# Context rows loaded later, spare matmuls before the head, transposes of a unit one gate tile sooner, gate rows inside the rope part

## The reference

```python
sh, sc, gt = jnp.split(cond @ w_mod[i] + b_mod[i], 3, axis=-1)           # modulation, latent; same for context
h_lat = x * (1.0 + sc[:, None]) + sh[:, None]
h_ctx = ctx * (1.0 + sc_c) + sh_c
q_dn, kv_dn, k_rope, gate = jnp.split(h @ w_in, MLA_SPLITS, axis=-1)     # the "head" (448 columns) and the gate (2048)
q = (_rmsnorm(q_dn, q_norm) @ w_uq).reshape(b, n, MLA_HEADS, MLA_NOPE + MLA_ROPE)
q_pos = jnp.concatenate([qa, _apply_rope(qr, cs[:, None], sn[:, None])], axis=-1)
# 16 heads: scores against 256 latent and 256 context keys, softmax, values, w_uv, times silu(gate), w_out
x = _layernorm(DEEPNORM_ALPHA * x + gt[:, None] * y_lat, ln_g[i], ln_b[i])
```

## Time and profile before

| | |
|---|---|
| median of three runs | 1565.81 us (1564.36 to 1566.65) |
| the profiled execution | 1564.42 us |
| its span, first to last instruction | 1562.5 us |
| mean granted TensorE clock | 0.996 |
| VectorE, ScalarE, GpSimd busy | 56%, 26%, 36% |
| bytes moved by DMA | 272.99 MB, mean 175 GB/s |

### The profile page before, as it was taken

One profiled execution on the slowest core, in us unless ns is written; L12 is line 12 of the kernel. 1 busy time (PEld: TensorE's weight loads), 2 busy tenths in 40 slices (PEclk: granted clock), 3 DMA queues, 4 the chain that ended last, 5 costly groups with the idle time before them and its releaser, 6 DMA issues.

```text
span 1562.5 us, 25477 instructions
## 1 busy us (share of the span) xinstructions
PE 1499.3 (96%) x10192; PEld 1127.4 (72%) x10192; DVE 872.9 (56%) x1745; ACT 402.4 (26%) x956; POOL 565.9 (36%) x412
## 2 busy tenths in 40 slices
PE   4999999999999999999998999999999999999998
PEld 3455556666655568898877888886788874688887
DVE  5879955454578978378576222253533332265642
ACT  1222243333312122332233011000223550232210
POOL 5013340000003303101103977783486201477774
PEclk9999999999999999999999999999999999999999
DMA  9856780130486636838585555554544123455441
GB/s 332 217 182 194 244 269 16 46 116 14 158 259 204 224 136 181 309 136 323 211 304 210 185 175 175 170 183 160 198 162 161 56 108 108 141 178 163 165 148 68
DMA packets 172605, 272.99 MB, mean 175 GB/s; under 512 B 51405, under 2 KB 85304, under 8 KB 171208
## 3 DMA queue, kind: packets, MB, share of 16 engines
q1 hardware_dynamic: 146096, 201.08, 38.1%
q0 software_dynamic: 16512, 42.49, 8.5%
q10 hardware_dynamic: 9880, 27.78, 4.9%
HBM read 228.26 MB, written 42.99 MB: 174 GB/s over the span
## 4 chain that ended last, share of the span: by engine, by line
PE 90%; DMA 4%; DVE 3%; ACT 1%; issue 1%; POOL 0%; SPq 0%; DVEq 0%; ACTq 0%; POOLq 0%
PE bank L499 84%; PE bank L502 6%; DMA memory<-in_w_mod 1%; DMA memory<-mc_scratch 1%; DMA memory<-in_mla_w_in 1%; DMA memory<-in_mla_w_uv 1%; DVE memory L2418 0%; DVE memory L2425 0%; DVE memory L2422 0%; DVE memory L2419 0%; DVE memory L2575 0%; ACT memory L1515 0%; ACT memory L1739 0%; DVE memory L2570 0%; ACT memory L1591 0%
## 5 line engine op out<-in xcount | busy, mean ns | idle before, releaser
L499 PE MATMUL bank<-memory 128*128 128x256 f32 (+8 forms) x9244 | 1402.3, 354 | 38.3 <-DMA memory<-in_w_mod 8.2
L499 PEld LDWEIGHTS bank<-memory 128*128 128x128 f32 (+4 forms) x9244 | 1021.8, 165 | 373.9 <-issue 246.1
L2784 POOL DMA_DIRECT2D mc_scratch<-memory x32 | 28.0, 876 | 498.9 <-DVE memory L2139 441.1
L502 PEld LDWEIGHTS bank<-memory 128*128 128x128 f32 (+1 forms) x948 | 107.9, 141 | 56.9 <-issue 33.6
L502 PE MATMUL bank<-memory 128*128 128x128 f32 (+1 forms) x948 | 124.3, 275 | 21.0 <-ACT memory L1359 9.0
L2823 POOL TENSOR_TENSOR memory<-memory 128x1024 f32<-128x1024 f32 (+1 forms) x34 | 80.9, 2380 | 143.0 <-PE bank L499 95.8
L2809 POOL DMA_DIRECT2D memory<-mc_scratch x32 | 17.3, 543 | 189.3 <-PE bank L499 189.3
L2825 POOL TENSOR_TENSOR memory<-memory 128x1024 f32<-128x1024 f32 (+1 forms) x34 | 81.0, 2382 | 2.7
L2790 POOL DMA_DIRECT2D k_scratch<-memory x128 | 76.5, 630 | 12.7 <-ACT memory L1432 12.3
L2828 POOL TENSOR_TENSOR memory<-memory 128x1024 f32<-128x1024 f32 (+1 forms) x34 | 80.0, 2353 | 2.7
L2826 POOL TENSOR_TENSOR memory<-memory 128x1024 f32<-128x1024 f32 (+1 forms) x34 | 80.5, 2368 | 0.0
(11 more groups left out here) (305 smaller groups left out, 1286.2 us busy)
## 6 DMA issues: line engine op xcount, KB each, us to landing
memory<-in_s_w_glu SPq DMA_DIRECT2D x32, 1024.0 KB, 7.6
memory<-in_w_mod SPq DMA_DIRECT2D x12, 2048.0 KB, 14.1
memory<-in_w_ffn_up SPq DMA_DIRECT2D x22, 1024.0 KB, 7.0
memory<-in_w_in SPq DMA_DIRECT2D x10, 2048.0 KB, 8.0
mc_scratch<-memory POOLq DMA_DIRECT2D x32, 512.0 KB, 4.5
mb_scratch<-memory ACTq DMA_DIRECT2D x32, 512.0 KB, 3.8
memory<-mb_scratch SPq DMA_DIRECT2D x32, 512.0 KB, 6.9
memory<-mc_scratch POOLq DMA_DIRECT2D x32, 512.0 KB, 6.3
```

The costliest lines, as they stand in the source:

```text
L499: return nc.tensor.matmul(o, l, r, start=start, stop=stop, skip_group_check=free)
L502: return nc.tensor.transpose(o, i, ident[0:n, 0:n])
L2784: pool.dma_start(mc_dram[u], over(mc[:, u % 3, GS:GS + 1], (144, 8), (1, P))).then_inc(*S.up("mc_out%d" % (u % 3), u, by=16))
```

## The change

- The two loads of ctx go from ACT's queue to SP's, behind `head_in`. The context's transposes, copies and modulation move behind head tile 0 on TensorE and ScalarE, and behind part of the tables on VectorE. They use banks 0, 1, 6 and 7 in place of the next in turn, which also shifts the banks of what follows; the second transposition of C, into bank 3, now follows the transposed D row there. The transposes of C come after head tile 1 in place of 2.
- `kept_busy(3)` and `kept_busy(5)`: spare products of the identity with 256 columns of x into bank 7, which nothing reads, behind the poles and behind mod column 3.
- Unit u is turned and stored behind gate tile u + 1 in place of u + 2; unit 14 thus comes before mod column 5's transpose.
- The four gate rows of the first layer go from in front of unit 15 into the first rope part. The waits for `ckvT` and `krT` go behind it.
- In the second rope part value product 5 and the latent values of head 6 stand between its steps, in place of behind it.

The core of the diff; ScalarE's program follows TensorE's order in the same way:

```diff
             mod_product(0, 0)
             x_transposes(0, 0)
             mod_product(0, 1)
             mod_turned(0, 0)
-            x_transposes(0, 1)
             mod_product(0, 2)
             mod_turned(0, 1)
             poles_turned()
+            kept_busy(3)
             mod_product(0, 3)
             mod_turned(0, 2)
             mod_turned(0, 3)
+            kept_busy(5)
...
-                if t == 2:
+                if t == 0:
+                    x_transposes(0, 1)
+                if t == 1:
                     for ql in range(2):
                         c_turned(0, ql, 2 + ql)
...
+            def kept_busy(n):
+
+                b = bank(pe, ("busy", n), [], 7)
+                for _ in range(n):
+                    mm(b[:, 0:T], ident, x[:, 0, 0:T], True, True, True)
...
-                    b = bank(pe, ("xT", l, c, k2), [freed], 4 + k2 if l else None)
+                    b = bank(pe, ("xT", l, c, k2), [freed], 4 + k2 if l else ((0, 1, 6, 7)[k2] if c else None))
...
-                if n >= 2:
-                    unit_turned(n - 2)
+                if n >= 1:
+                    unit_turned(n - 1)
...
-            unit_turned(14)
...
-            gate_rows(0)
             unit_turned(15)
             for i in range(2):
                 pe.wait_ge(*S.at("qnT", i))
-            pe.wait_ge(*S.at("ckvT"))
-            pe.wait_ge(*S.at("krT"))
...
                 projected(0)
                 projected(1)
+                if hf == 0:
+                    gate_row(0, 0, 0)
                 plain(0)
                 projected(2)
                 plain(1)
+                if hf == 0:
+                    gate_row(0, 0, 1)
                 rotated(0)
                 projected(3)
+                if hf == 0:
+                    gate_row(0, 1, 0)
+                else:
+                    value_up(H // 2 - 3)
                 plain(2)
+                if hf == 0:
+                    gate_row(0, 1, 1)
                 rotated(1)
+                if hf:
+                    latent_values(H // 2 - 2)
                 plain(3)
...
-                if h >= 2:
+                if h >= 2 and h + 1 != H // 2:
                     value_up(h - 2)
-                if 1 <= h <= H:
+                if 1 <= h <= H and h + 1 != H // 2:
                     latent_values(h - 1)
...
# VectorE
-            for c in range(2):
-                modulated(0, c)
+            modulated(0, 0)
             powers(pow1, pow_t)
...
+                if r == 0:
+                    modulated(0, 1)
...
# SP
             ring("head_in")
+            for t in range(2):
+                sp.dma_start(x[:, 2 + t, :], a["ctx"][0, t * P:(t + 1) * P, :]).then_inc(*S.up("x_in%d" % (2 + t), by=16))
             b_load(0)
```

More of the change, by code:

```diff
@@ L521, in mod_turned, with gate_row @@
                 tr(b[:, 0:P], modrow[:, ct % 2, :]).then_inc(*S.up("modT_mm", (l, ct)))
[L523 to L531, removed]
+            def gate_row(l, n, c):
+                pe.wait_ge(*S.at("shsc", (l, 4 + n)))
+                b = bank(pe, ("gtb", l, n, c), [("gtb", (l, n, c))], 4 + n if l else None)
+                for i in range(4):
+                    column_ = shsc[:, l, 2 * KD + 4 * n + i, c:c + 1]
+                    last = mm(b[:, i * P:(i + 1) * P], over(column_, (0, P)), ident, i == 0, i == 3, True)
+                last.then_inc(*S.up("gtb_mm", (l, n, c)))
             def x_transposes(l, c):
@@ L706, in qk_head @@
                 if h == 0:
+                    pe.wait_ge(*S.at("ckvT"))
+                    pe.wait_ge(*S.at("krT"))
                     pe.wait_ge(*S.at("wukv"))
@@ L989, in _ @@
             y_turned(3)
-            gate_rows(1)
+            for n in range(2):
+                gate_row(1, n, 0)
             def product(o, left, right, start, stop):
@@ L1345, in _ @@
             act.dma_start(ident, a["c_ident"][0]).then_inc(*S.up("ident", by=16))
[L1346 to L1351, removed]
+            for t in range(2):
+                act.dma_start(x[:, t, :], a["x"][0, t * P:(t + 1) * P, :]).then_inc(*S.up("x_in%d" % t, by=16))
             act.wait_ge(*S.at("bmod_zero"))
@@ L1355, in _ @@
                 act.dma_start(bmod[32 * j:32 * j + 2, :, :], src).then_inc(*S.up("bmod", by=16))
-            x_load(2)
-            x_load(3)
             act.wait_ge(*S.at("cond_in"))
@@ L1370, in _, with gate_row @@
             A(sc_a[:, 7, :], sc_a[:, 2, :], ACT.Sin, scale=0.5).then_inc(*S.up("sin", 1))
[L1371 to L1378, removed]
+            def gate_row(l, n, c):
+                act.wait_ge(*S.at("gtb_mm", (l, n, c)))
+                if l == 1:
+                    act.wait_ge(*S.at("res0", (1, 3)))
+                A(gtb[:, c, n * 512:(n + 1) * 512], at_bank("gtb", l, n, c), ACT.Copy).then_inc(*S.up("gtb", (l, n, c)))
             def modulated(l, c):
@@ L1434, in _ @@
             for t in range(NTT):
-                if t == 3:
+                if t == 1:
+                    turned_copies(1)
+                    modulated(0, 1)
+                if t == 2:
                     for ql in range(2):
@@ L1449, in _ @@
                 A(gT[:, f, :], at_bank("gate", f), ACT.Silu).then_inc(*S.up("gate", f))
-                if f >= 2:
-                    unit_stored(f - 2)
+                if f >= 1:
+                    unit_stored(f - 1)
                 if f == 7:
@@ L1454, in _ @@
                         c_conjugated(1, ql)
-            unit_stored(14)
             for u in (12, 13):
```

## The result

The changed kernel takes 1577.12 us in the median of four runs (1575.26 to 1580.06), the kernel before 1566.23 (1564.36 to 1567.84). The ratio is 1.0075, with a 95% interval of 1.0057 to 1.0094: slower by 0.75%, some 11 us. Slower was forecast, but by 3.7 us; the measured time lies above the range.

What follows compares the result with a forecast made beforehand. TensorE, busy 96% of the span, was taken as the bound, with DMA limiting the start to 41.06 us. Terms +0.5 + 1.5 + 1.7 + 0 = +3.7 us gave 1569.5; 8-in-10 range 1565.2 to 1571.8.

Steps and rivals of the forecast that it cites:

- the order of the units: Gate part, up to mod column 5's transpose: +0.87 us for unit 14 turned earlier and +1.8 for two waits.
- a start that gained less: Everything up to the first gate tile: forecast to sum to -2.15 us.
- Head's weight: Start: with the context loads behind it, the weight lands at 38.15 us, -2.9 us.
- Spare matmuls: Before the head: they keep the clock full for head tile 0, -1.8 us, bounds 0 and -1.8.
- The context's transposes and dtab: Between head tiles, then C's second transposition: +1.75 us for 16 transposes, +0.8 for TensorE's new wait for dtab.
- Units 9 and 11: Behind gate tiles 10 and 12: TensorE waits 0.9 us each for VectorE, together +1.8, bounds 0 and 2.
- ScalarE's copies and the stores behind them ... wait for nothing new: Gate part: ScalarE's work moves along with the transposes and adds no wait.
- Hand-over of unit 15: VectorE hands it over 7.8 us after mod column 5's transpose, no later relative to it; TensorE idles 6.1 us.
- The clock behind it: After the pause before unit 15, TensorE's half clock costs +1.7 us, bounds 0 and 2.5.
- Gate rows in the rope part: First rope part becomes 12.9 us, longer than the 11.3 us load of wukv: +1.5 us, bounds 0.7 and 2.5.
- Second rope part: A covered 0.76 us wait against a new wait before head 8's scores: 0 us, bounds -0.8 and +0.8.
- Everything the change touches lies in the first 330 us: Whole program: the prediction read only this stretch in order of time as touched by the change.

Runs made afterwards that it cites:

- the last experiment: The mends without the eight spare matmuls before the head: 1563.41 us against 1565.59 for the kernel before, ratio 0.9982.
- the mends: Changed kernel with VectorE's units 9, 11, 15 earlier, C's second transposition in bank 1, ScalarE's C copies before unit 6's store, old second rope part: 1561.85 us.
- units alone: Kernel before with only unit u turned and stored behind gate tile u + 1: 1571.97 us against 1565.66, ratio 1.0047.
- units 9 and 11 moved: Changed kernel with VectorE's unit 9 before mod row 4, unit 11 before mod column 4, unit 15 before mod column 5: 1566.30 us, ratio 0.9998.
- gate rows alone: Kernel before with only the four gate rows moved into the first rope part: 1569.47 us against 1565.66, ratio 1.0027.
- the start alone: Changed kernel with units, gate rows and second rope part as in the kernel before: 1562.88 us against 1565.66, ratio 0.9988.

## Why the prediction was wrong in size

The prediction was 3.7 us and the span grew by 11.0. Of the 7.3 between them, 3.2 come from the order of the units, 1.0 from the clock, 1.0 from the gate rows, 0.5 from the second rope part, 0.5 from a start that gained less, and 1.1 from a place where the prediction didn't look.

- **Head's weight: the time right, the reason in part wrong.** The head began at 38.26 (41.10 before), forecast 38.15. The weight had landed at 37.6 (issued at 23.4, 14.2 us on its way). What released the head was ScalarE's modulation, which follows mod 3's product; the two were forecast 0.5 us apart and I named the wrong one. The match is partly luck: with the same loads the head began at 39.6 to 40.9 in three other profiles, in which mod 3's product or the spare matmuls ahead of it ran at half clock.
- **Spare matmuls, about right for head tile 0:** 1.8 forecast, 1.6 by the rows of the last experiment. That the three in front can delay mod 3's product wasn't in the prediction.
- **The context's transposes and dtab, right:** 1.75 us for the transposes (44.34 to 46.09), and a wait for dtab of 0.80 us, both as forecast. Gate tile 0 began 1.7 us sooner, forecast 2.15.
- **Units 9 and 11, right:** waits of 0.97 and 1.02 us, forecast 0.9 each; each also costs 0.2 at the restart (1.09 us for eight transposes in place of 0.87).
- **"ScalarE's copies and the stores behind them ... wait for nothing new": this step failed.** Behind gate tile 7 ScalarE now stores unit 6, an even unit, with its block diagonal (L1423), where it stored unit 5. C's copy stands behind that on ScalarE's queue. ScalarE's timeline of the changed kernel:

```profile
130.37 0.60 ACT L1461 ACTIVATE memory<-bank 128x512 f32<-128x512 f32 x1 [6.59 <-PE bank L499]
130.99 0.85 ACT L1423 ACTIVATE memory<-memory 64x256 f32<-64x256 f32 x2
131.87 1.08 ACT L1433 ACTIVATE memory<-bank 128x512 f32<-128x512 f32 x2
132.99 0.33 ACTq L1435 DMA_DIRECT2D mb_scratch<-memory  x1
133.36 0.66 ACT L1410 ACTIVATE memory<-bank 128x256 f32<-128x256 f32 x2 [0.40 <-ACT memory L1433]
```

  TensorE had its second transposition ready to go and waited 2.52 us for the last of these, against 0.84 before, and no kernels of a pair stand in between any more: 1.7 us.
- **Kernels and gate tiles, missing.** A gate tile directly behind a pair's kernels costs 0.19 us more (8.12 us for 1.06 + 6.87, the 88.51 row), and this neighbourhood occurs 7 times in place of 1. That would be 1.1 us, but transposes behind the kernels had paid something too. In the chain of the kernel before, four of them take 0.60 us there, where four others take 0.44:

```profile
131.71 0.60 PE bank L502 x4
...
321.76 0.44 PE bank L502 x4
```

  So 0.9 us is left. With 0.9 for unit 14, 2.4 for the two waits with their restarts, 1.7 and 0.9 the order of the units costs 5.9 us, as the chain has it, more than twice the forecast 2.7.
- **Hand-over of unit 15, right:** 7.9 us behind mod column 5, forecast 7.8, with a pause of 5.7 (6.1 forecast).
- **The clock behind it: mechanism right, term too small.** 2.7 us, forecast 1.7 with a bound of 2.5. I took the loss of head tile 0 as the nearest row. There half clock ended 3 us into the tile; here it lasted for 6 us.
- **Gate rows in the rope part: too small.** 5.2 - 2.7 = 2.5 us, forecast 1.5. The gate rows bring 3.4 us and remove 0.76 + 0.79 of waits; the third of them brought a wait of 0.4, as its bank is that of the second projection, which VectorE was still rotating, and a restart.
- **Second rope part: +0.5,** forecast 0 with a bound of 0.8.
- **"Everything the change touches lies in the first 330 us": this failed too.** The banks given out in turn shifted for the whole program, and near 1100 us that costs 1.1 us. No run gives those transposes another bank, so the mends still pay it.

The errors have one sign. Each of my terms had been priced as the pure work moved or the one wait seen; what each shift did to the neighbours in the queue wasn't gone through on ScalarE, and what it did to the banks only as far as dtab.

## What to carry to other kernels

To ask for a result one step sooner, go through every engine that stands between producer and consumer, not the producer alone: what is now queued ahead of each copy, and which small step it holds up. When work is moved out of a pause, first find what makes the pause; here it was one small step in front of unit 15 on VectorE, and moving that was worth 8 us. With unit 15 in time the place of the gate rows was worth only 0.3 us, where moving them alone had cost 4.2. A spare matmul that keeps the clock is free only where no product with a successor stands behind it: at half clock three of them put mod 3's product off. Where buffers are handed out in turn by one count, dropping a turn at the start moves every later one; compare the buffer numbers of both programs to the end.

## What the runs showed of the hardware

- A pause of 2.52 us at C's transposition stands in five profiles. In two of them TensorE's clock came down behind it (units alone: 0.71 of full speed from 137 to 141 us; units 9 and 11 moved: 0.57 from 134 to 138), in the other three it stayed full (the changed kernel's: 1.00 from 100 to 150 us). The four runs of the changed kernel spread over 4.8 us, those of before over 3.5.
- After a pause of 5.7 us TensorE worked at half clock for some 6 us (216 to 222), twice as long as in head tile 0 of the kernel before; at 4.5 us of pause (gate rows alone) the clock was 0.50 as well, from 213 to 216.
- The head's start varied between 38.2 and 40.9 us among eight kernels with the same program up to there: six lie at 38.2 to 38.7, one at 39.9 and one at 40.9. In both late ones the three spare matmuls ran at half clock (0.50 from 31.4 to 34.0 us in the one at 39.9, where they started when they did in the start alone); in the one at 40.9 they also started later, behind b_mod.
- Between 591.30 and 853.92 us of the kernel before (262.6 us) no edit of this study touches the order of the work, and yet the 14 profiles differ there by 4 us (261.0 to 265.0). A single profile's total therefore doesn't show a difference of a microsecond or two; the stretch with the change in it does.
- A gate tile directly behind a pair's kernels (products of 32 columns of weights) took 0.19 us more than behind transposes, in all seven places of the changed kernel.
